# A delta-rule stage: the diagonal blocks are cut on GpSimd, the level-one subtraction moves to VectorE, and TensorE's head loop is no longer unrolled

## The reference, cut to what matters

```python
kb = k * beta[..., None]
lower = jnp.where(strict, jnp.einsum('bhncd,bhnmd->bhncm', kb, k) * decay, 0.0)
rhs = jnp.concatenate([v * beta[..., None], kb * jnp.exp(gc)[..., None]], axis=-1)
sol = lax.linalg.triangular_solve(jnp.eye(C) + lower, rhs, left_side=True, lower=True)
u, w = sol[..., :dv], sol[..., dv:]
qk = jnp.einsum('bhncd,bhnmd->bhncm', q, k) * decay
...
def step(S, inp):                     # one chunk of tokens after the other
    v_new = u_i - w_i @ S
    o_i = qd_i @ S + qk_i @ v_new
    S = S * gt_i + kd_i.T @ v_new
```

## Time and profile before

| what | value |
|---|---|
| median of 3 runs (lowest to highest) | 3435.66 us (3433.48 to 3437.10) |
| the profiled execution, its own time | 3437.1 us |
| its span in the trace | 3435.4 us |
| TensorE busy | 3314.3 us, 96% |
| VectorE, ScalarE, GpSimd busy | 54%, 42%, 20% |
| the eight delta heads in the trace | 1706.0 to 2421.5 us |

### The profile page before, as it was taken

How to read it: one execution, slowest core, us unless ns; L and a number is a source line. 1 busy time by engine, 2 the same in 40 slices (tenths; PEclk the granted TensorE clock), 3 DMA queues, 4 the chain that set the end, 5 groups by cost and what they waited for, 6 DMA issues and landing times. The chain is left out here.

```text
span 3435.4 us, 70539 instructions
## 1 busy us (share of the span) xinstructions
PE 3314.3 (96%) x28074; PEld 3136.1 (91%) x28074; DVE 1868.7 (54%) x3332; ACT 1459.7 (42%) x3057; POOL 696.4 (20%) x645
## 2 busy tenths in 40 slices
PE   7999999998999999999999999998999899999998
PEld 7999999997888888877788989988999899999998
DVE  6655565764555455544445555554441865556555
ACT  5222235555555555443344444444323722223444
POOL 2323310102122222000022222222001333221000
PEclk9999999999999999999999999999999999999999
DMA  5222236732222222389311111114522322224664
GB/s 165 75 78 84 82 121 218 234 124 70 69 69 69 70 69 69 121 305 379 106 42 44 52 51 52 52 51 130 164 81 75 119 81 82 75 75 147 201 195 141
DMA packets 351893, 385.45 MB, mean 112 GB/s; under 512 B 22492, under 2 KB 259110, under 8 KB 351422
## 3 DMA queue, kind: packets, MB, share of 16 engines
q1 hardware_dynamic: 341606, 347.78, 32.4%
q0 software_dynamic: 9888, 32.88, 2.7%
q10 hardware_dynamic: 84, 0.35, 0.0%
HBM read 305.53 MB, written 75.40 MB: 111 GB/s over the span
## 5 line engine op out<-in xcount | busy, mean ns | idle before, releaser
L673 PE MATMUL ps<-p_hi,w_hi 128*128 128x352 f32 x912 | 304.5, 334 | 2.3 <-PEq L123 1.4
L673 PE MATMUL ps<-p_hi,w_lo 128*128 128x352 f32 x912 | 294.1, 322 | 0.0
L673 PE MATMUL ps<-p_lo,w_hi 128*128 128x352 f32 x912 | 293.4, 322 | 0.0
L1999 PE MATMUL ps<-p_hi,w_hi 128*128 128x352 f32 x840 | 285.6, 340 | 0.0
L1999 PE MATMUL ps<-p_lo,w_hi 128*128 128x352 f32 x840 | 281.9, 336 | 0.2 <-issue 0.2
L1999 PE MATMUL ps<-p_hi,w_lo 128*128 128x352 f32 x840 | 280.8, 334 | 0.0
L673 PEld LDWEIGHTS ps<-p_hi,w_hi 128*128 128x128 f32 x912 | 172.2, 189 | 4.1 <-issue 1.7
L2840 PE MATMUL ps<-op_hid_hi,w_hi 128*128 128x384 f32 (+1 forms) x528 | 170.8, 324 | 4.1 <-DVE w_lo L2515 2.3
L2840 PE MATMUL ps<-f_hid_hi,w_hi 128*128 128x352 f32 x528 | 171.3, 325 | 1.6 <-DVE w_lo L2515 1.5
L673 PEld LDWEIGHTS ps<-p_lo,w_hi 128*128 128x128 f32 x912 | 172.6, 189 | 0.0
L673 PEld LDWEIGHTS ps<-p_hi,w_lo 128*128 128x128 f32 x912 | 171.7, 188 | 0.0
(11 more groups left out here) (698 smaller groups left out, 10354.8 us busy)
## 6 DMA issues: line engine op xcount, KB each, us to landing
w_raw<-in_ffn_w_out_dram SPq DMA_DIRECT2D x136, 256.0 KB, 3.4
w_raw<-in_w_in_dram SPq DMA_DIRECT2D x67, 512.0 KB, 4.0
sa_v<-in_cache_v_dram SPq DMA_DIRECT2D x120, 256.0 KB, 6.7
w_raw<-in_ffn_w_in_dram SPq DMA_DIRECT2D x48, 512.0 KB, 5.1
sa_k<-in_cache_k_dram SPq DMA_DIRECT2D x72, 256.0 KB, 5.5
f_s<-in_ffn_w_out_dram SPq DMA_DIRECT2D x64, 256.0 KB, 3.5
pair_s<-in_ffn_w_out_dram SPq DMA_DIRECT2D x64, 256.0 KB, 3.4
d_hid<-f_gb SPq DMA_DIRECT2D x44, 264.0 KB, 2.1
```

The costliest lines, as they stand in the source:

```text
L673: mm = nc.tensor.matmul(m.ps[:, bank, 0:CH], a[:, k, w], b[:, f, cols(c)], start=(f == 0 and i == 0), stop=(f == KT - 1 and i == 2))
L1999: mm = nc.tensor.matmul(m.ps[:, (k + c) % 2, 0:CH], a[:, k, f * P:(f + 1) * P], x[:, f, cols(c)], start=(j == 0), stop=(j == len(terms) - 1))
```

## The change

Four things change, all in `delta_heads`:

1. ScalarE no longer cuts the diagonal blocks; GpSimd does, at the head of its function `diagonal(x)`, which takes the place of `masks(x)`.
2. The subtraction from the identity goes from GpSimd to VectorE (`turned(1, x)`). VectorE's order is now: gather, `product(h, 2, 1)`, `products` of all nine tiles, `turned(1, 0)`, `base(0)`, `product(h, 2, 2)`, `turned(1, 1)`, `base(1)`, `product(h, 2, 3)`. GpSimd's `kp` no longer waits for `conv_done`.
3. TensorE issues `grams(4)` ahead of the piece q2, and waits for all nine `qk_done` ahead of the levels.
4. TensorE runs its heads through `schedule`, with the hardware loop over h = 1 to 5.

```diff
 ScalarE, head
-                take(h, "q", 0)
-                take(h, "q", 1)
-                for x in range(2):
-                    tiles = slice(4 * x, 4 * x + 4)
-                    act.wait_ge(low_done, NT * h + 4 * x + 4)
-                    if x == 0:
-                        wait(act, r_mm, 12 * h)
-                    for b in range(4):
-                        rows = slice(SUB * b, SUB * b + SUB)
-                        nc.scalar.copy(lo_d[rows, tiles, :], lo_t[rows, tiles, rows]).then_inc(cut_done, 1)
-                take(h, "q", 2)
+                for c in range(3):
+                    take(h, "q", c)
 VectorE, head
                 gather(h, 2)
-                for t in range(TT):
+                product(h, 2, 1)
+                for t in range(NT):
                     products(t)
...
+                    if lev == 1:
+                        dve.wait_ge(mask_done, 4 * h + 2 * x + 1)
+                        if x == 0:
+                            wait(dve, s_mm_s, 2 * h)
+                            if isinstance(h, int) and h == 0:
+                                dve.wait_ge(s_stored, 48)
+                        ids = m.cst[:, C_IDS:C_IDS + SUB].rearrange("p (o d) -> p o d", o=1).to_broadcast([P, 4, SUB])
+                        nc.vector.tensor_tensor(ttc[:, tiles, :], ids, mk[:, x, 0, :, :], ALU.subtract).then_inc(u_turned, 1)
...
+                turned(1, 0)
                 base(0)
-                product(h, 2, 1)
-                products(TT)
                 product(h, 2, 2)
                 if not more:
                     row_low(2)
+                turned(1, 1)
                 base(1)
 GpSimd, head
-                def masks(x):
+                def diagonal(x):
                     tiles = slice(4 * x, 4 * x + 4)
-                    pool.wait_ge(cut_done, 8 * h + 4 * x + 4)
+                    pool.wait_ge(low_done, NT * h + 4 * x + 4)
                     if x == 0:
                         wait(pool, r_mm, 12 * h)
-                        if isinstance(h, int) and h == 0:
-                            pool.wait_ge(s_stored, 48)
+                        pool.wait_ge(tri_done, 3 * h + 3)
+                    else:
+                        pool.wait_ge(mask_done, 4 * h + 2)
+                        wait(pool, u_turned, NTURN * h)
+                    pool.nop(nofuse=True)
+                    for b in range(4):
+                        rows = slice(SUB * b, SUB * b + SUB)
+                        nc.gpsimd.tensor_copy(lo_d[rows, tiles, :], lo_t[rows, tiles, rows]).then_inc(cut_done, 1)
+                    pool.wait_ge(cut_done, 8 * h + 4 * x + 4)
                     nc.gpsimd.tensor_tensor(mk[:, x, 0, :, :], lo_d[:, tiles, :], first, ALU.mult).then_inc(mask_done, 1)
-                    pool.wait_ge(mask_done, 4 * h + 2 * x + 1)
-                    nc.gpsimd.tensor_tensor(ttc[:, tiles, :], ids, mk[:, x, 0, :, :], ALU.subtract).then_inc(u_turned, 1)
...
                 pool.wait_ge(scales, 4 * h + 4)
-                pool.wait_ge(conv_done, 12 * h + 12)
                 nc.gpsimd.tensor_tensor(kp[:, :, :], tok[:, :, 1, :], by_scale(BPE), ALU.mult).then_inc(kp_done, 1)
 TensorE, head
                 piece(h, "q", 1)
+                grams(4)
                 piece(h, "q", 2)
-                grams(4)
                 piece(h, "z", 0)
-                pe.wait_ge(qk_done, NT * h + TT)
+                pe.wait_ge(qk_done, NT * h + NT)
...
-                        wait_small((mask_s, 2 * h + 2), (qk_done, NT * h + NT))
+                        wait_small((mask_s, 2 * h + 2))
 TensorE, program
-            first()
-            for h in range(H):
-                head(h)
+            schedule(pe, first, head, lambda: None)
```

More of the change, by code:

```diff
@@ L1798, in turned @@
                     tiles = slice(4 * x, 4 * x + 4)
-                    dve.wait_ge(u_done, 14 * h + 2 * (lev - 1) + x + 1)
-                    nc.vector.transpose(ttc[:, tiles, :].rearrange("p k d -> p (k d)"),
-                                        uc[:, tiles, :].rearrange("p k d -> p (k d)")).then_inc(u_turned, 1)
+                    if lev == 1:
[7 more added lines that the diff above has]
+                    else:
+                        dve.wait_ge(u_done, 14 * h + 2 * (lev - 1) + x + 1)
+                        nc.vector.transpose(ttc[:, tiles, :].rearrange("p k d -> p (k d)"),
+                                            uc[:, tiles, :].rearrange("p k d -> p (k d)")).then_inc(u_turned, 1)
+                turned(1, 0)
                 base(0)
-                product(h, 2, 1)
-                products(TT)
                 product(h, 2, 2)
@@ L1895, in head @@
                 nc.gpsimd.tensor_tensor(qk_t[0:NS, TT, 0:NS], lo_t[0:NS, TT, 0:NS], m.cst[0:NS, C_TRI4:C_TRI4 + NS], ALU.mult).then_inc(tri_done, 1)
-                def masks(x):
+                def diagonal(x):
                     tiles = slice(4 * x, 4 * x + 4)
-                    pool.wait_ge(cut_done, 8 * h + 4 * x + 4)
+                    pool.wait_ge(low_done, NT * h + 4 * x + 4)
                     if x == 0:
                         wait(pool, r_mm, 12 * h)
-                        if isinstance(h, int) and h == 0:
-                            pool.wait_ge(s_stored, 48)
+                        pool.wait_ge(tri_done, 3 * h + 3)
+                    else:
+                        pool.wait_ge(mask_done, 4 * h + 2)
[5 more added lines that the diff above has]
+                    pool.wait_ge(cut_done, 8 * h + 4 * x + 4)
                     first = m.cst[:, C_LEV:C_LEV + SUB].rearrange("p (o d) -> p o d", o=1).to_broadcast([P, 4, SUB])
                     nc.gpsimd.tensor_tensor(mk[:, x, 0, :, :], lo_d[:, tiles, :], first, ALU.mult).then_inc(mask_done, 1)
-                    pool.wait_ge(mask_done, 4 * h + 2 * x + 1)
-                    ids = m.cst[:, C_IDS:C_IDS + SUB].rearrange("p (o d) -> p o d", o=1).to_broadcast([P, 4, SUB])
-                    nc.gpsimd.tensor_tensor(ttc[:, tiles, :], ids, mk[:, x, 0, :, :], ALU.subtract).then_inc(u_turned, 1)
                     k = LEVELS - 3
@@ L1924, in put @@
                         nc.gpsimd.tensor_copy(uu[rows, tiles, rows], uc[rows, tiles, :]).then_inc(put_done, 1)
-                masks(0)
-                masks(1)
+                diagonal(0)
+                diagonal(1)
                 pool.wait_ge(low_done, NT * h + NT)
```

## The result

| what | before | after |
|---|---|---|
| median (lowest to highest; 4 runs each, same chip) | 3434.57 us (3430.48 to 3437.10) | 3480.37 us (3477.10 to 3482.59) |
| span of the profiled execution | 3435.4 us | 3478.1 us |
| granted TensorE clock, mean | 0.984 | 0.977 |

The ratio of after to before is 1.0134, with a 95% interval of [1.0116, 1.0151]: +46 us, where +16.5 was forecast and 3470 us was the top of the range. The direction is as forecast; the size is not.

The account below looks back on a forecast made before the run. TensorE was taken to bound the kernel, busy 3314.3 of 3435.4 us. Terms 10.3 + 2.1 + 1.2 + 0.9 + 2.0 = +16.5 us on 3437.1 gave 3453.6, 3452 us as a median; range 3442 to 3470.

Parts of the forecast that it names:

- the wait before `kp` removed: GpSimd before kp: dropping the conv_done wait costs nothing; upper bound 2.10 us in each of seven heads.
- product, grams, cut, subtraction: Delta heads: +2.1 us for the earlier product and grams(4), +1.2 us for the moved cut and subtraction.
- jumps and registers: TensorE's loop: four taken branches +10.3 us, semaphore values worked out from h 0.4 us a head, +2.0 us.
- The cut on GpSimd, the subtraction on VectorE: Last mask 1.4 to 2 us later; TensorE waits 0.4 us at the levels in heads 0, 1 and 6: +1.2 us.
- Rival B: Waits in the levels decide: kp overtakes the last convolution product, 2.10 us in seven heads, or "issue" doubles; 3466 us, chance 0.17.
- The clock: TensorE at half clock after some jumps; a full stretch is worth 1.6 us, called the loosest part.
- The jump: TensorE's loop, four taken branches: 3.0 us each less 0.42 us of ScalarE lateness covered, +10.3 us; bounds 7.5 to 15.6.
- The product and grams(4): TensorE waits 1.0 us at grams(4), 0.7 on average in heads 0, 1 and 6, none in 2 to 5: +2.1 us.
- Head 7: TensorE's 5.45 us wait hangs on when GpSimd gets to wq: +0.9 us, bounds -1 and +2.5.
- The later wait for `qk_done`: TensorE ahead of the levels: costs nothing, as the ninth product is done some 4 us earlier.
- Rival C: Whole loop body stays in TensorE's instruction memory: jumps cheap, issue waits in heads 2 to 5 go; -4.4 us, 3431, chance 0.06.

Follow-up runs that it names:

- e1_wait_back: The changed kernel with GpSimd's wait for conv_done before kp put back; median 3447.64 us, ratio 1.0039 to the kernel before.
- e11_cut_wait_off: The kernel before with only the cut on GpSimd and the subtraction on VectorE, and without the conv_done wait before kp; 3477.12 us, ratio 1.0119.
- e10_cut_only: The kernel before with only the cut moved to GpSimd and the subtraction to VectorE, the conv_done wait kept; 3444.93 us, ratio 1.0026.
- e2_unrolled: The changed kernel with TensorE's eight heads written out again instead of looped; 3482.43 us, ratio 1.0145 to the kernel before.
- e5_both_back: The changed kernel with the conv_done wait before kp put back and TensorE's heads written out; 3440.62 us, ratio 1.0031 to the kernel before.
- e4_wait_off: The kernel before with GpSimd's wait for conv_done before kp taken out; 3436.45 us, ratio 1.0005.
- e3_loop_only: The kernel before with only TensorE's heads put through the hardware loop; 3445.38 us, ratio 1.0033.
- e7_grams_back: The changed kernel with the conv_done wait back, TensorE's heads written out and grams(4) again behind q2; 3443.76 us, ratio 1.0033 to the kernel before.
- e6_gaps: The changed kernel with GpSimd also waiting for its own kp before q_t and its own q_t before wq; 3442.61 us, ratio 1.0027 to the kernel before.

## Why the prediction was wrong

| part | forecast | measured |
|---|---|---|
| the wait before `kp` removed | 0 | +33 (after against `e1_wait_back`), +32 (`e11_cut_wait_off` against `e10_cut_only`), +39 (`e2_unrolled` against `e5_both_back`); 0 on the kernel before (`e4_wait_off`) |
| product, grams, cut, subtraction | +3.3 (and 0.9 in head 7) | about +10 (`e5_both_back`), +9 for cut and subtraction (`e10_cut_only`) |
| jumps and registers | +10.3, +2.0 | +11 alone (`e3_loop_only`), +3 and -4 on top of the other parts (`e1_wait_back` less `e5_both_back`, after less `e2_unrolled`), both within the intervals |

**The step that failed** is the paragraph "The cut on GpSimd, the subtraction on VectorE", where the removed wait for `conv_done` was priced at nothing, with 2.10 us a head, the length of `kp`, as its upper bound. Two things in it were wrong. First, it put the overtaking at nothing because GpSimd gets later by the copies and `kp` had started when TensorE was two microseconds into the levels. That compares `kp` with TensorE's place and not with VectorE's. `product(h, 2, 3)` begins 1 us before the last mask operation ends in the kernel before (1998.85 against 1999.82), and the subtraction on VectorE, which the prediction priced only as a wait of TensorE, uses that up. Secondly, the bound took one GpSimd operation as the most that can stand before the product. What is behind the removed wait is a queue of four (`kp`, `q_t`, `wq`, `kd`), 6.7 us long. Rival B had the place and the mechanism, that `kp` takes the memory first; its price was 2.10 where the trace shows 4.9 to 5.1 of idle time and half clock after it. Its sign, that `kp` starts before the product, cannot be read off the recorded starts: they are 2014.76 and 2014.74, and the lateness shows in the product's length. By four operations its price would have been 2.10 + 2.34 + 0.24 + 2.10 less what VectorE has in hand.

**The clock** was expected at half after some of the jumps. It was after one of four, and after every one of the seven stalls, which the sum did not have. Of the stage's 50 us, 31.7 are idle time and 18.4 are work done slower. The length of an idle time alone does not tell what follows: after 2.52 us TensorE went on at full clock, after 2.48 us in the same execution and after 2.30 us in the earlier trace rows at half.

**The jump** was right as a duration (3.3 to 3.8 us a branch, 2.0 to 2.5 us idle) and too dear as a term beside the other parts; alone it came to +11, near the +12.3 of jumps and registers. The sum took 0.42 us of cover from it; what it covers is also the wait of `grams(4)` (0.86 a head), and "issue" in the levels: 14.7 us in the kernel before (8.6 before L2140, the rest before L2126 and L2129). In `e3_loop_only` it is 7.2 before these lines, and 4.7 more stand before pieces (L1999: 14.1 us in ten waits, 9.4 of them the jumps), 11.9 together. The forecast let it cover the first in heads 2 to 5, but did not let it cover the "issue" waits. Why those shrink is not shown.

**The product and grams(4)**: the wait of 1.0 us in head 1 came as 0.87, in heads 6 and 7 as 0.45, in head 0 as 0.11, and not at all in 2 to 5, as said: 1.9 us against 2.1.

**The cut and the subtraction** were mis-sized at 1.2 us. The trace shows `dl_uc` of L1770 waited for in the changed kernel by 2.9 us under the cover of grams and jumps, and by 8.4 to 11 us without that cover (`e7_grams_back`, `e10_cut_only`). In head 3 the short subtraction took 1.31 and 1.35 us on VectorE beside GpSimd's mask operation; on GpSimd it had been 0.46 in the first half. The longest subtraction of the 16 took 1.365 us, the shortest 0.371. That is what the Trainium skill, "SBUF — State Buffer", section "SBUF: two separate sides", gave, and the prediction had set it aside as unproven; by it the term would have been 5. That page of the Trainium skill has each engine hold the memory for one whole instruction. The run of 7.85 us shows more: between four operations that stood end to end the waiting engine got no turn.

**Head 7** came out 1.4 us shorter (4.0 for 5.45) instead of 0.9 longer, because `q_t` and `wq` did not wait for the product: with the wait back it is 5.4 again (`e1_wait_back`). **The later wait for `qk_done`** cost nothing, as said. Rival C fell with the branches.

**What stays open**: where `e3_loop_only` loses the part of its 11 us that the one traced execution, at its high clock, does not show; whether the subtraction alone, without the cut on GpSimd, would bring the stall; and why the product gets its turn between the last mask and `mk_s`, which also stand end to end (`e4_wait_off`), but not between `kp`, `q_t`, `wq` and `kd`. The number of waits in GpSimd's code does not settle it. There are two ahead of `mk_s` and one ahead of `kp`, `q_t` and `wq`, but one also stands ahead of the second half's first mask operation of the kernel before (`cut_done`, met at 1995.03), and there the product of 1994.64 did get its turn, and the mask operation took 1.51 us instead of 0.47:

```profile
1995.56 1.51 POOL L1906 TENSOR_TENSOR dl_mk<-dl_lo_d,cst 128x128 f32<-128x128 f32 x1
```

The waits that `e6_gaps` adds differ from these in that GpSimd waits for its own operation that has only just ended.

## What to carry to other kernels

A wait that is always met by the time it is reached may still be what orders two engines on a shared resource. Price its removal by the whole queue behind it, not by the first instruction, and by the place of the rival instruction after the rest of the change: here it was worth nothing before VectorE's chain became 1.4 us later, and 32 to 39 us afterwards.

A stall of the bounding engine covers other waits, so its cost in an otherwise late kernel can be less than alone (the jumps: +11 alone, nothing measurable beside the other parts). And a stall may be paid a second time at half clock, as all seven of 4.9 to 5.1 us were here; look at the pace of the matmuls behind it.

## What the runs showed of the hardware that was not expected

VectorE's 128 x 1080 product beside GpSimd, over all 72 of the changed kernel (ns, min/median/max):

```profile
L1608 DVE SCALAR_TENSOR_TENSOR dl_cs<-dl_xc,conv_weight,dl_cs x72: 1302/1344/7854, 1679.6 to 2396.7; 128x1080 f32<-128x1080 f32 x72
```

The VectorE product that met the run of four GpSimd operations waited for the whole run, 6.5 us for 1.3 us of work, in each of the eight heads. A wait of GpSimd on its own last operation was enough to end this (`e6_gaps`, 3.26 us). TensorE's clock was at half for 4.7 to 10.6 us after each of the seven idle times of 4.9 to 5.1 us; after those of 2.0 to 2.5 us at the eight jumps of two kernels it was at half twice. A taken branch of TensorE took 3.3 to 3.8 us, some 60 times VectorE's 56 ns in the same loop, and about a third of it was covered by queued work.
